# A sixth Strassen pair in each layer's mix, a fused mask and maximum, and a new order of steps, in a two-layer decoder trunk on one core

## The chip, the core and the metric

The kernel runs on one core of one Trainium2 chip. It is timed as a whole: device microseconds from its start to its end, median of three runs. One more execution was taken with the hardware profiler, and everything that is said of engines below comes from that one.

## What is computed

Two layers run on 256 tokens of width 1024, in float32. Each layer does this (norms, gains and masks left out of the sketch):

```python
x += 1/2 * swiglu(rmsnorm(x), w1, w3, w2)            # first feed-forward block, hidden width 2816
h  = rmsnorm(x); P = h @ w_in                         # one projection, cut into rq rk rv rg | sq sk sv | mq | gates
ret = retention(rq, rk, rv) * silu(rg)                # branch A, 4 heads
swa = sliding_window_attention(sq, sk, sv, sinks)     # branch B, 16 query heads of 64, window 128, a sink per head
mo  = memory_attention(mq, mk, mv)                    # branch C, mk and mv from rmsnorm(mem) @ w_mem_kv
x += (g0 * (ret @ w_ur) + g1 * (swa @ w_us) + g2 * (mo @ w_um)) @ w_o
x += 1/2 * swiglu(rmsnorm(x), ...)                    # second feed-forward block
```

In the sliding window attention a score is s = (q.k) / 8 plus a mask of 0 or -1e30. The maximum m of a row is taken over its scores and the head's sink; then come exp(s - m), the row's sum with exp(sink - m) added, and the division.

## The kernel before

**Precision.** A float32 product is made of three TensorE passes. Each operand is split in a rounded part (hi) and the rest (lo), and hi*lo, hi*hi and lo*hi are summed (three_passes, L777 to L779). ScalarE makes w_hi from the raw weights (L1184), VectorE makes w_lo = raw - w_hi (L1586), each in two halves of 1024 columns. A weight unit is 128x2048 numbers, 1 MB.

**Items.** The work is one long list of items. A plain unit (for instance mv0.1: memory values, column half 0, row half 1) is 8 (tile, block) places times 3 passes, 24 matmuls of 512 columns. Two plain chunks of one width can instead be a pair, done by Strassen's method (the Winograd form) in seven products (rk:5, rk:1, and so on), each of 12 matmuls; done as plain units the pair takes 96 matmuls, as products 84. Products 5, 6, 7 and 4 need a sum of weight quarters. Such a sum is made by VectorE in the raw buffer (L1583, a 128x2048 addition), or, where the table ADDED names it, by an accumulating DMA issued from GpSimd (L714). A product also needs its own rounding and its own rest, as a unit does, so that a pair needs 7 of these where plain units need 4. Products 3, 5, 6 and 7 read sums of the activations (S_hi, S_lo), made once in each block.

**The ring.** In the mix the rounded weights lie in three places (w_hi, w_lo), taken in turn. So the place for item o comes free when TensorE has finished item o-3: after item X of the list, ScalarE rounds item X+3 and VectorE then makes its rest. Raw weights lie in three places of their own, and some other buffers are lent to them while they are idle (RAW_B, RAW_Q, RAW_X, RAW_A); their loads go through SyncE's queue in list order.

**The order.** SCHEDULE is one string, written out by hand, and all engines walk through it in the same order. For each entry ScalarE and VectorE first evacuate that item's result from its PSUM bank and then do the split that is due behind it. Entries without a dot or colon are steps: `sqt` transposes the attention queries; `s0` to `s3` are the scores of four heads each; `e0` is the exponentials on ScalarE, `n0` the division on VectorE; `pt0` and `pv0` are the transposes and products with the values; `rotq` and `rotk` are the rotations; `S_sum`, `S_hi`, `S_lo` make the activation sums of the mix; `mkt` transposes the memory keys.

**Banks.** Steps take the PSUM banks 4 to 7 in rotation. A score step takes all four, so two score steps with no other step of this kind between them use the same four banks, and TensorE waits for all four before the first matmul of a score step:

```python
for j in range(4):
    pe.wait_ge(*room(l, f"s{g}_{j}"))
```

The transposes `sqt` wait for all of the query chunks' evacuations (`wait_done("sq0", "sq1")`) before the first of them.

**Before the change** five pairs run in each mix (rk, rg, gs, gr, gm). The queries of the local attention are four plain units (sq0.0, sq0.1, sq1.0, sq1.1).

Of the kernel before, what the change touches and what calls it, by code (L numbers as in the profile page):

```python
# [119 lines left out]
ADDED = {(0, 'gm'): (6, 7, 4), (0, 'gr'): (7, 4), (0, 'gs'): (6, 7), (0, 'rg'): (6, 7, 4), (0, 'rk'): (6, 7, 4), (1, 0): (7, 4), (1, 1): (6, 7, 4), (1, 2): (7,), (1, 3): (6, 7, 4), (2, 0): (7, 4), (2, 1): (6, 7, 4), (2, 2): (7, 4), (2, 3): (7,)}  # L120
# [42 lines left out]
def item_of(o):  # L163
    return ITEMS[o // NI][o % NI]
# [25 lines left out]
RAW_B, RAW_Q, RAW_X, RAW_A = (3, 4), (5, 6), 7, 8  # L190
# [32 lines left out]
def plan_weights():  # L223
# [26 lines left out]
    loads, raw_of, held = [], {}, [(-1, None)] * (RAW_A + 1)  # L250
    added_after, added_at, adds, sum_behind = [[] for _ in range(n)], {}, {m: 0 for m in (5, 6, 7, 4)}, {}
    for o in range(n):
# [3 lines left out]
        else:  # L256
# [22 lines left out]
        for unit, key, until in parts:  # L279
            s = min(raw_slots(o), key=lambda v: held[v][0])  # L280
# [9 lines left out]
DVE_STEPS = 28  # L290
# [88 lines left out]
def build(nc, x_in, mem_in, memt_in, stream, gains_in, gfin_in, rot_in, decay_in, mask_in, ident_in, out):  # L379
# [6 lines left out]
    with ctx:  # L386
# [42 lines left out]
        hM = new("hM", [P, KT, SEQ], at=q_at)  # L429
# [1600 lines left out]
```

## Time and profile before

| what | value |
|---|---|
| median of 3 runs | 1439.35 us (1438.45 to 1440.83) |
| the profiled execution, its time | 1438.82 us |
| its span, first to last instruction | 1436.8 us |
| TensorE busy | 1418.4 us |
| VectorE busy | 1170.3 us |
| ScalarE busy | 973.0 us |
| GpSimd busy | 67.9 us |
| granted TensorE clock | 0.998 |

The 2.0 us between the time and the span lie outside of the first and last instruction. Busy time is a union of instruction times. Matmuls overlap in the pipeline, so the distance from start to start is what a matmul costs.

### The profile page before, as it was taken

What the parts mean: (1) busy time and instruction counts of PE and PEld (TensorE: products, weight loads), DVE (VectorE), ACT (ScalarE), POOL (GpSimd) and SP (SyncE); (2) the same over time, 40 slices, a digit from 0 to 9 for tenths busy, and PEclk for the clock granted to TensorE, in tenths of its full rate; (3) what the DMA queues carried; (4) which work ended last, traced back from release to release, by engine and by line L of the source; (5) the groups of instructions that cost most, each with busy time, mean ns of one, the idle gap of its engine ahead of it and who ended that gap; (6) DMA issues with size and microseconds to landing.
All of it is one profiled execution on the core that took longest, in us unless ns stands there. A gap on an engine that the chain in (4) does not pass through costs nothing.

```text
span 1436.8 us, 17632 instructions
## 1 busy us (share of the span) xinstructions
PE 1418.4 (99%) x6654; PEld 1164.8 (81%) x6654; DVE 1170.3 (81%) x1322; ACT 973.0 (68%) x1426; POOL 67.9 (5%) x93
## 2 busy tenths in 40 slices
PE   8999999999999999999999999999999999999997
PEld 6887888878888888888887888887788888888886
DVE  7999756799868769898799987468997778688895
ACT  6777666879656747676577675668785666577663
POOL 0000000000000000000000000000000000000000
PEclk9999999999999999999999999999999999999999
DMA  9998748688668675998849787486785886859861
GB/s 369 269 285 247 265 146 299 195 258 228 204 199 257 233 299 201 280 279 245 278 138 271 260 211 262 172 269 208 224 240 204 248 245 211 325 164 311 254 206 44
DMA packets 49395, 341.39 MB, mean 238 GB/s; under 512 B 5568, under 2 KB 6208, under 8 KB 8608
## 3 DMA queue, kind: packets, MB, share of 16 engines
q1 hardware_dynamic: 37392, 259.54, 48.2%
q0 software_dynamic: 8912, 63.84, 23.4%
q10 hardware_dynamic: 3008, 16.90, 3.0%
q8 instruction: 53, 0.87, 0.2%
q14 instruction: 30, 0.25, 0.0%
HBM read 332.91 MB, written 7.34 MB: 237 GB/s over the span
## 4 chain that ended last, share of the span: by engine, by line
PE 83%; DVE 9%; DMA 4%; issue 2%; ACT 1%; SPq 0%; ACTq 0%; DVEq 0%; POOLq 0%
PE bank L777 25%; PE bank L779 25%; PE bank L778 25%; DVE w_lo L1586 5%; PE bank L834 3%; DMA raw_b<-in_stream 2%; DMA raw<-in_stream 1%; DVE w_lo_more L1586 1%; PE bank L1111 1%; PE bank L1093 1%; PE bank L985 1%; PE bank L997 1%; ACT w_hi L1184 1%; PE bank L1012 1%; DVE raw L1583 1%
## 5 line engine op out<-in xcount | busy, mean ns | idle before, releaser
L1586 DVE TENSOR_TENSOR w_lo<-raw,w_hi 128x1024 fp32r<-128x1024 f32 x338 | 398.1, 1221 | 122.5 <-ACT w_hi L1184 122.0
L1184 ACT ACTIVATE w_hi<-raw 128x1024 fp32r<-128x1024 f32 x338 | 338.9, 1054 | 145.7 <-PE bank L779 130.2
L777 PE MATMUL bank<-w_hi,hT_lo 128*128 128x512 f32 (+1 forms) x684 | 267.9, 392 | 1.3 <-DVE half L1691 1.0
L779 PE MATMUL bank<-w_lo,hT_hi 128*128 128x512 f32 (+1 forms) x684 | 263.4, 385 | 0.0
L778 PE MATMUL bank<-w_hi,hT_hi 128*128 128x512 f32 (+1 forms) x684 | 263.3, 385 | 0.0
L777 PEld LDWEIGHTS bank<-w_hi,hT_lo 128*128 128x128 f32 x684 | 128.6, 188 | 32.1 <-issue 4.2
L777 PE MATMUL bank<-w_hi,S_lo 128*128 128x512 f32 x372 | 148.6, 400 | 1.2 <-ACT snap L1267 1.2
L779 PEld LDWEIGHTS bank<-w_lo,hT_hi 128*128 128x128 f32 x684 | 128.5, 188 | 26.2
L778 PEld LDWEIGHTS bank<-w_hi,hT_hi 128*128 128x128 f32 x684 | 128.7, 188 | 23.9
L779 PE MATMUL bank<-w_lo,S_hi 128*128 128x512 f32 x372 | 145.1, 390 | 0.0
L778 PE MATMUL bank<-w_hi,S_hi 128*128 128x512 f32 x372 | 144.9, 390 | 0.0
L777 PE MATMUL bank<-w_hi,bT_lo 128*128 128x512 f32 x320 | 125.9, 393 | 0.0
L779 PE MATMUL bank<-w_lo,bT_hi 128*128 128x512 f32 x320 | 124.7, 390 | 0.0
L778 PE MATMUL bank<-w_hi,bT_hi 128*128 128x512 f32 x320 | 124.6, 389 | 0.0
L777 PE MATMUL bank<-w_hi,gT_lo 128*128 128x512 f32 x248 | 97.5, 393 | 1.1 <-DVE gT_lo L1604 1.0
L779 PE MATMUL bank<-w_lo,gT_hi 128*128 128x512 f32 x248 | 96.7, 390 | 0.0
L778 PE MATMUL bank<-w_hi,gT_hi 128*128 128x512 f32 x248 | 96.5, 389 | 0.0
L1586 DVE TENSOR_TENSOR w_lo<-raw_q,w_hi 128x1024 fp32r<-128x1024 f32 x78 | 92.0, 1223 | 5.0 <-ACT w_hi L1184 5.0
L1184 ACT ACTIVATE w_hi<-raw_q 128x1024 fp32r<-128x1024 f32 x78 | 78.3, 1055 | 24.4 <-PE bank L779 16.5
L777 PEld LDWEIGHTS bank<-w_hi,S_lo 128*128 128x128 f32 x372 | 69.9, 188 | 15.8 <-ACT snap L1267 2.1
L779 PEld LDWEIGHTS bank<-w_lo,S_hi 128*128 128x128 f32 x372 | 69.8, 188 | 15.0
L778 PEld LDWEIGHTS bank<-w_hi,S_hi 128*128 128x128 f32 x372 | 70.0, 188 | 13.7
(231 smaller groups left out, 2460.7 us busy)
## 6 DMA issues: line engine op xcount, KB each, us to landing
raw<-in_stream SPq DMA_DIRECT2D x149, 1024.0 KB, 5.8
raw_q<-in_stream SPq DMA_DIRECT2D x34, 1024.0 KB, 7.1
raw_b<-in_stream SPq DMA_DIRECT2D x31, 1024.0 KB, 7.3
raw<-in_stream POOLq DMA_DIRECT2D x29, 1024.0 KB, 8.5
raw_x<-in_stream SPq DMA_DIRECT2D x18, 1024.0 KB, 4.9
raw_b<-in_stream POOLq DMA_DIRECT2D x14, 1024.0 KB, 10.3
raw_a<-in_stream SPq DMA_DIRECT2D x12, 1024.0 KB, 6.8
raw_q<-in_stream POOLq DMA_DIRECT2D x9, 1024.0 KB, 10.9
```

What stands on the lines that cost most here:

```text
L777: nc.tensor.matmul(dst, xl, wh[:, a:b], start=first, stop=False, skip_group_check=more)
L778: nc.tensor.matmul(dst, xh, wh[:, a:b], start=False, stop=False, skip_group_check=more)
L779: return nc.tensor.matmul(dst, xh, wl[:, a:b], start=False, stop=last, skip_group_check=more)
L834: last = nc.tensor.transpose(bank(name)[:, at:at + P], src(t, k0 + j), ident[:, :])
L985: last = nc.tensor.matmul(bank(name)[:, i * n:(i + 1) * n], sqT[rows, head // 2, tokens(b)], skT[rows, head // (SWA_H // SWA_KV), 0:n], st ...
L997: last = nc.tensor.transpose(bank(name)[:, i * P:(i + 1) * P], prob[:, g % 2, head, part * P:(part + 1) * P], ident[:, :])
L1012: nc.tensor.matmul(o, v, heads[:, :, odd, 0:2, :], start=True, stop=False, skip_group_check=True)
L1093: last = nc.tensor.matmul(bank(name)[:, t * MEM:(t + 1) * MEM], mqT[:, 2 * h + k, tokens(t)], mkT[:, 2 * h + k, :], start=k == 0, stop=k == 1)
L1111: last = nc.tensor.matmul(bank(name)[:, j * SEQ:(j + 1) * SEQ], mv[:, m, k * P:(k + 1) * P], mpT[:, h, m, :], start=m == 0, stop=m == 1)
L1184: nc.scalar.activation(slots(o)[0][:, part], raw_slot(s)[:, part], ACT.Copy).then_inc(hi_split, 1)
L1583: nc.vector.tensor_tensor(raw_slot(to[0]), raw_slot(to[0]), raw_slot(plus[0]), ALU.add).then_inc(weights_made, 1)
L1586: nc.vector.tensor_tensor(lo[:, part], raw_slot(s)[:, part], hi[:, part].bitcast(F32), ALU.subtract)\
```

## The change

The pair sq (its chunks sq0 and sq1) becomes a sixth pair. Only one of its sums, that of product 7, goes by DMA; those of 5, 6 and 4 are made by VectorE. Two sums of other pairs also move from DMA to VectorE in each layer (rk:6 in both layers, gm:4 in both layers). The units of mv move ahead, among the products of sq. The four stretches of mask, scale and maximum are fused: one tensor_tensor_reduce for each head and block does the scaling, adds the mask, and gives the row's maximum with the sink as its start value. Both raw_q places are lent to the first part of the mix, and a new place raw_s (over srg, after `re`) to its last part. hM moves from the raw_q region to that of sqT. Two waits are added in the feed-forward blocks before act_s and act_g are written again; both name work of the chunk before.

```diff
-mk0.1+xt0 mk1.0+xt1 skv.0 mk1.1 sq0.0 S_sum S_hi S_lo mkt sq0.1 sq1.0 skt sq1.1 mv0.0 sqt rk:5 s0 mv0.1 rk:3 e0 s1 mv1.0 mv1.1 e1 n0 n1 rk:1 rv0.0 pt0 rk:6 pv0 pt1 rk:7 mv_out rk:2 s2 rk:4 rg:5 pv1 e2 n2 rotq rv0.1 s3 rv1.0 rg:3 rqt rg:1 pt2 e3 rotk rg:6 rg:2 pv2 rv1.1 rg:7 n3 mq1.0 rkt rg:4 gs:5 pt3 gs:3 rs ...
+mk0.1+xt0 mk1.0+xt1 S_sum mk1.1 skv.0 mkt S_hi S_lo mv0.0 sq:5 sq:1 sq:3 sq:6 mv0.1 mv1.0 mv1.1 skt sq:7 sq:2 sq:4 sqt rk:5 s0 rk:3 e0 s1 n0 rk:1 e1 n1 rv0.0 pt0 rk:6 pv0 mv_out pt1 rk:7 rk:2 s2 rk:4 rg:5 pv1 rg:3 rv0.1 e2 s3 n2 rotq rv1.0 rg:1 pt2 e3 rg:6 rqt rotk rg:2 rv1.1 rg:7 pv2 rkt n3 mq1.0 rg:4 gs:5 pt3 gs:1 gs:3 rs ...
-ADDED = {(0, 'gm'): (6, 7, 4), ..., (0, 'rk'): (6, 7, 4), ...}
+ADDED = {(0, 'gm'): (6, 7), ..., (0, 'rk'): (7, 4), (0, 'sq'): (7,), ...}
+Q_ITEMS = {RAW_Q[0]: (AT[0]["mix", 0] + 3, min(AT[0]["mix", UNIT_AT[c, 1]] for c in ("mv0", "mv1")) + 1),
+           RAW_Q[1]: (AT[0]["mix", 0] + 3, RV_ITEM + 1)}
+S_ITEMS = item_after("re") + 2, item_after("mpt")
@@ sync: loads into lent places wait for the work that used them
+                if s == RAW_Q[0] and part_of(item) == 0 and not again and o < NI:
+                    sp.wait_ge(mem_msq_ready, TT)
+                if s == RAW_Q[1] and part_of(item) == 0 and not again:
+                    sp.wait_ge(memt_lo, o // NI + 1)
+                if s == RAW_S and (owner is None or o // NI != owner // NI):
+                    sp.wait_ge(*out_of(o // NI, "ro_3"))
@@ feed-forward, ScalarE and VectorE
+                            if behind is not None:
+                                act.wait_ge(*out_of(l, f"up{f}_{behind}t{t}"))
+                        if behind is not None:
+                            dve.wait_ge(*full(l, f"gt{f}_{behind}"))
@@ VectorE, steps s0 to s3
-                            nc.vector.scalar_tensor_tensor(dst, src, HD ** -0.5, msk, op0=ALU.mult, op1=ALU.add)\
-                                .then_inc(free(name), 1)
+                            for i in range(2):
+                                head, at = 2 * i + odd, G_SINK + GRP * g + 2 * i + odd
+                                last = nc.vector.tensor_tensor_reduce(
+                                    pr[:, head, 0:WIN] if b == 0 else pr[:, head, WIN:3 * WIN], bank(name)[:, i * w:(i + 1) * w],
+                                    mask[:, WIN:] if b == 0 else mask[:, :], HD ** -0.5, gains[:, l, at:at + 1],
+                                    ALU.add, ALU.max, smax[:, par, head, b:b + 1])
+                            last.then_inc(free(name), 1)
-                        nc.vector.tensor_reduce(smax[:, par, :, 0], pr[:, :, 0:WIN], axis=AXX, op=ALU.max)
-                        own(nc.vector.tensor_reduce(smax[:, par, :, 1], pr[:, :, WIN:3 * WIN], axis=AXX, op=ALU.max))
-                        settled()
-                        own(nc.vector.tensor_tensor(smax[:, par], smax[:, par], sink, ALU.max))
-                        settled()
```

## Rows read from the trace of the kernel before

**Rows 1.** Part 1 of the page: busy us, share of span, instructions

```profile
PE 1418.4 (99%) x6654; PEld 1164.8 (81%) x6654; DVE 1170.3 (81%) x1322; ACT 973.0 (68%) x1426; POOL 67.9 (5%) x93
```

**Rows 2.** Busy time by stretch: length, then PE, PEld, DVE, ACT, POOL, clock, DMA

```profile
0.00:190.50 190.50, 183.04 (x818) 147.58 (x819) 159.41 (x176) 127.89 (x171) 11.28 (x22) 1.00 0.86 281
190.50:243.90 53.40, 53.40 (x278) 45.50 (x277) 34.11 (x37) 38.18 (x62) 2.40 (x6) 1.00 0.60 229
243.90:353.40 109.50, 109.44 (x554) 86.99 (x553) 95.92 (x126) 86.00 (x158) 5.66 (x7) 1.00 0.78 228
353.40:543.90 190.50, 190.50 (x893) 159.05 (x892) 144.47 (x170) 118.84 (x173) 7.03 (x8) 1.00 0.74 242
720.70:899.20 178.50, 176.63 (x796) 144.53 (x797) 155.43 (x165) 123.34 (x163) 9.43 (x11) 1.00 0.76 230
952.60:1062.10 109.50, 109.44 (x553) 86.98 (x552) 95.89 (x125) 85.96 (x158) 5.70 (x7) 1.00 0.79 228
```

**Rows 3.** Timeline of TensorE, layer 0: end of mv0.0, sqt, rk:5, s0, mv0.1

```profile
249.09 0.39 PE L779 MATMUL bank<-w_lo,bT_hi 128*128 128x512 f32 x1
249.32 1.91 PE L834 MATMUL bank<-ident,stB 128*128 128x128 f32 x16
250.99 0.48 PE L777 MATMUL bank<-w_hi,S_lo 128*128 128x512 f32 x1
...
253.35 0.39 PE L778 MATMUL bank<-w_hi,S_hi 128*128 128x512 f32 x1
253.58 0.39 PE L779 MATMUL bank<-w_lo,S_hi 128*128 128x512 f32 x1
253.90 1.58 PE L985 MATMUL bank<-skT,sqT 64*128 64x128 f32 x16
255.41 0.50 PE L777 MATMUL bank<-w_hi,bT_lo 128*128 128x512 f32 x1
```

**Rows 4.** Timeline, ScalarE and VectorE behind rk:5, and s1 on TensorE

```profile
254.00 0.69 ACT L1396 ACTIVATE stB<-bank,rstd 128x512 f32<-128x512 f32 x1 [0.47 <-PE bank L779]
254.59 2.00 ACT L1184 ACTIVATE w_hi<-raw 128x1024 fp32r<-128x1024 f32 x2
255.67 2.36 DVE L1586 TENSOR_TENSOR w_lo<-raw,w_hi 128x1024 fp32r<-128x1024 f32 x2 [2.64 <-ACT w_hi L1184]
257.95 1.94 DVE L1849 SCALAR_TENSOR_TENSOR prob<-bank,mask 128x256 f32<-128x256 f32 x4
260.02 0.69 DVE L1853 TENSOR_REDUCE smax<-prob 128x4 f32<-128x512 f32 x1
260.63 1.21 DVE L1854 TENSOR_REDUCE smax<-prob 128x4 f32<-128x1024 f32 x1
261.87 0.17 DVE L1857 TENSOR_TENSOR smax<-smax,gains 128x8 f32<-128x8 f32 x1
262.07 0.17 DVE L1859 TENSOR_SCALAR snm<-smax 128x8 f32<-128x8 f32 x1
262.15 0.16 DVE L1860 TENSOR_TENSOR ssink<-gains,smax 128x8 f32<-128x8 f32 x1
263.47 0.39 PE L779 MATMUL bank<-w_lo,S_hi 128*128 128x512 f32 x1
263.79 1.58 PE L985 MATMUL bank<-skT,sqT 64*128 64x128 f32 x16
```

**Rows 5.** Timeline: TensorE waits for a bank that ScalarE copies out

```profile
47.11 0.39 PE L779 MATMUL bank<-w_lo,S_hi 128*128 128x512 f32 x1
48.19 0.50 PE L777 MATMUL bank<-w_hi_more,S_lo 128*128 128x512 f32 x1 [0.69 <-ACT snap L1267]
47.54 0.60 ACT L1267 ACTIVATE snap<-bank 128x512 f32<-128x512 f32 x1 [0.23 <-PE bank L779]
```

**Rows 6.** Groups by form on VectorE, 243.9 to 351.2: busy us, mean ns

```profile
L1586 DVE TENSOR_TENSOR w_lo<-raw,w_hi 128x1024 fp32r<-128x1024 f32 x27 | 31.8, 1220 | 8.8 <-ACT w_hi L1184 8.8
L1849 DVE SCALAR_TENSOR_TENSOR prob<-bank,mask 128x512 f32<-128x512 f32 x8 | 5.1, 684 | 0.0
L1849 DVE SCALAR_TENSOR_TENSOR prob<-bank,mask 128x256 f32<-128x256 f32 x8 | 3.0, 418 | 0.0
L1583 DVE TENSOR_TENSOR raw<-raw,raw_a 128x2048 f32<-128x2048 f32 x1 | 2.3, 2284 | 0.0
L1797 DVE SCALAR_TENSOR_TENSOR stB<-bank,minus_rstd,stB 128x512 f32<-128x512 f32 x2 | 1.5, 748 | 0.0
```

**Rows 7.** Timeline of VectorE: short operations from PSUM, back to back

```profile
362.12 0.42 DVE L1879 TENSOR_TENSOR sdec<-bank,decay 128x256 f32<-128x256 f32 x1
362.45 0.28 DVE L1880 TENSOR_TENSOR sdec<-bank,decay 128x128 f32<-128x128 f32 x1
362.65 0.42 DVE L1879 TENSOR_TENSOR sdec<-bank,decay 128x256 f32<-128x256 f32 x1
```

**Rows 8.** Timeline of ScalarE: exponentials that also give a row sum

```profile
268.30 0.49 ACT L1488 ACTIVATE prob<-prob,snm 128x256 f32<-128x256 f32 x1
268.69 0.19 ACT L1488 ACTIVATION_READ_ACCUMULATOR prob<-prob,snm 128x1 f32 x1
268.79 0.39 ACT L1488 ACTIVATE prob<-prob,snm 128x128 f32<-128x128 f32 x1
```

**Rows 9.** Part 6 of the page: DMA issues, KB each, median us to landing

```profile
raw_q<-in_stream SPq DMA_DIRECT2D x34, 1024.0 KB, 7.1
raw<-in_stream POOLq DMA_DIRECT2D x29, 1024.0 KB, 8.5
```

**Rows 10.** Groups by form on ScalarE, 243.9 to 353.4: evacuations

```profile
L1337 ACT ACTIVATE stB<-bank,rstd 128x512 f32<-128x512 f32 x1 | 0.7, 689 | 1.9 <-PE bank L779 1.9
L1405 ACT ACTIVATE stB<-bank,rstd 128x512 f32<-128x512 f32 x1 | 0.7, 689 | 2.4 <-PE bank L779 2.4
```

More of the change, by code:

```diff
@@ L216, in raw_slots @@
         slots.append(RAW_A)
+    if PAIRS[0] and part_of(item_of(o)) == 0:
+        slots += [s for s in RAW_Q if Q_ITEMS[s][0] < i < Q_ITEMS[s][1]]
+    if PAIRS[0] and S_ITEMS[0] < i < S_ITEMS[1]:
+        slots.append(RAW_S)
     return slots
@@ L240, in plan_weights @@
     for o in range(n):
-        item = item_of(o)
-        if item[0] == "prod" and item[3] in SUMS and item[3] not in added(item):
+        l, item = o // NI, item_of(o)
+        if item[0] == "prod" and item[3] in SUMS and item[3] not in added(l, item):
             sums_first[o - SUM_EARLY.get(item[3], 1)].append((item[:3], item[3]))
@@ L262, in plan_weights @@
                 for p in SUMS:
-                    if p not in added(item) and SUMS[p] == q:
+                    if p not in added(l, item) and SUMS[p] == q:
                         until = max(until, sum_at[l, item[:3], p])
@@ L270, in plan_weights @@
                 for p in SUMS:
-                    if p not in added(item) and SUMS[p] == WEIGHT[m]:
+                    if p not in added(l, item) and SUMS[p] == WEIGHT[m]:
                         count = max(count, sum_at[l, item[:3], p])
                 sum_behind[l, item[:3], m] = count
-            if m in added(item):
+            if m in added(l, item):
                 adds[m] += 1
@@ L279, in plan_weights @@
         for unit, key, until in parts:
-            s = min(raw_slots(o), key=lambda v: held[v][0])
+            lent = {RAW_A: A_ITEMS, RAW_S: S_ITEMS, **Q_ITEMS, **dict.fromkeys(RAW_B, B_ITEMS)} if part_of(item) == 0 else {}
+            s = min([v for v in raw_slots(o) if v not in lent or until <= lo_at[l * NI + lent[v][1] - 1]], key=lambda v: held[v][0])
             loads.append((o, l * NU + unit, s, held[s], until))
@@ L610, in sums_no, with plain_behind @@
             return (2 + mix) * l + (0, 1 + mix)[f - 1] if f else 3 * l + 1
+        def plain_behind(l, f, c):
+            order = [s[2] for s in ffn_steps(l, f) if s[0] == "up" and s[3] == 1]
+            return order[order.index(c) - 1] if order.index(c) else None
         QUARTERS = {2: (0, 0), 6: (0, 1), 4: (1, 0), 7: (1, 1)}
```

41 lines of the change are left out of this document (26 added, 15 removed).

## The prediction

> **What bounds the kernel now.** I read the shares of busy time first, then busy time by stretch of the schedule, then the timeline at the places that the change touches. [Rows 1] show TensorE busy for 1418.4 of the 1436.8 us. Matmul times overlap, so I take the distance between starts: 253.35 to 253.58 is 0.23 us, and one product of 12 matmuls, rk:5, runs from 250.99 to about 253.80, where its last start (253.58) plus one step ends [rows 3]. Twelve steps of 0.227 us are 2.72 us, and a plain unit of 24 is 5.44 us. That step holds wherever two 512-wide matmuls follow each other with no wait between.
>
> By stretch [rows 2] the mix of layer 0 is full: 53.40 of 53.40, 109.44 of 109.50 and 190.50 of 190.50 us. TensorE is idle for 7.5 us in the first feed-forward block, where the kernel starts up, and for 1.9 us in that of layer 1. So in the mix there is next to no wait that any change could remove. What the change can win there is work taken from TensorE, and every new wait of TensorE in the mix is paid in full, because nothing later has slack to give back.
>
> The second thing to see in [rows 2] is VectorE. It is busy for 34.11 of 53.40 us before 243.9 and for 95.92 of 109.50 us from 243.9 to 353.4, where the local attention lies. Layer 1 repeats this to a tenth (95.89). The clock is 1.00 throughout.
>
> **What is removed from TensorE.** Four units (96 matmuls) become seven products (84). That is 12 x 0.227 = 2.72 us per layer, 5.44 us in all. No transposes and no activation sums are added: S_hi and S_lo are there for the other pairs.
>
> **What is added on VectorE for the pair.** Three more splits of two halves at 1.22 us each (2.36 us with their overlap [rows 4, 6]), three sums at 2.28 us and three evacuations at 0.75 us [rows 6]: 7.1 + 6.8 + 2.2 = 16.1 us per layer. They fall in the stretch where VectorE is idle for 53.40 - 34.11 = 19.3 us [rows 2]. TensorE gets 4 x 5.44 us of mv units there as well, against 4 x 2.36 us of VectorE, so on the whole the pair is hidden. Locally it is less roomy: between `skv.0` and sq:3 VectorE must do S_lo (about 2.5 us), the sum for sq:6 and two splits. By the same walk as below I find the rest for sq:3 about 0.4 us late.
>
> **The transposes of the queries.** Before, a whole unit (mv0.0) stood between the last query unit and sqt, and the timeline shows no gap at 249.32 [rows 3]. Now sqt stands right behind sq:4. TensorE has to wait for ScalarE to see the end of sq:4 (0.2 us, as 253.80 to 254.00 [rows 4]) and to copy 0.69 us [rows 10]. The nearest wait of this form in the trace is that at 47.11 to 48.19, start to start 1.08 us instead of 0.23, so 0.85 us lost, with a 0.60 us copy [rows 5]. With 0.69 us it is 0.95 us per layer, and 0.85 at least.
>
> **The second score step is where the sum is decided.** s0 and s1 take the same four banks, and s1 waits until all four are free. Before, TensorE had mv0.1 and rk:3 between them, 8.2 us. Now it has rk:3 alone. I count from the end of rk:5 (253.80). TensorE does s0 in 1.60 us (253.80 to 255.41 [rows 3]) and rk:3 in 2.72, and asks for s1 at +4.32. VectorE must first make the rest of item rk:5 + 3, and this waits for the ring place that rk:5 frees: ScalarE copies rk:5 out, rounds from +0.79 to +2.79, VectorE makes the rest, and it begins on the scores of s0 at +4.15 (257.95 [rows 4]). That chain is the same after the change, with rv0.0 in place of mv1.0. Queued behind it on VectorE are the masks, so the banks come free only at 4.15 + X, where X is the time of the masking.
>
> X was 1.95 us for four operations (257.95 to 259.89 [rows 4]); the maxima came behind the release of the banks. Now the maximum is inside: eight operations, four of 128 and four of 256 columns, and nothing is released before its second head is done. The trace does not show this operation. From below: plain operations of these two widths out of PSUM start 0.33 and 0.20 us apart [rows 7], so 4 x 0.53 = 2.1 us. From above: no overlap, the 256-wide one 0.42 us and the 128-wide one 0.28 us [rows 7], each with 0.06 us for a pointer operand (748 against 684 ns [rows 6]) and 0.17 us for reading the maximum out as a small operation of its own [rows 4]: 4 x 0.65 + 4 x 0.51 = 4.6 us. Between the two, ScalarE's exponentials are the nearest row, since they also write a per-row result: the read adds about 0.1 us to the step [rows 8]. With 0.1 us for the read and 0.06 for the pointer, X = 2.1 + 8 x 0.16 = 3.4 us. The wait is 4.15 + X + 0.1 for the restart - 4.32: 3.3 us per layer, between 2.0 and 4.5.
>
> The Trainium skill bears on X (VectorE: DVE Perf Modes, section "Two Vector instructions with no wait between them"): an operation that also writes out its accumulator is two instructions. By it a group has 8 + 8 + 2 = 18 VectorE instructions where it had 9, which speaks against the fusion. No row here shows such a pair on VectorE; on ScalarE the reading instruction is there [rows 8]. The same page ("The DRAIN you can't avoid") has the next operation start only when the pipeline is empty; here the next one starts 0.09 us before the end of the one before [rows 7], and the rows decide. By that page X would be 4 x (0.42 + 0.28) = 2.8 us without the reads.
>
> **The rest of the local attention.** A group's VectorE time goes from 4.29 us (257.95 to 262.31, less overlap [rows 4]) to X + 0.25 = 3.65, so 2.6 us less over four groups. Against that the sum for rk:6 comes from the DMA (2.2 us). Four mv units leave the stretch: 21.8 us of TensorE, but only 9.1 us of VectorE. So the stretch of 109.5 us becomes 87.7 us of TensorE and 95.9 - 9.1 + 2.2 - 2.6 = 86.4 us of VectorE. VectorE had 13.6 us of room and has 1.3, while it has unavoidable idle pieces such as the 2.64 us before its split in [rows 4]. The wait at s1 already gives it 3.3 us. I take 1.4 us per layer for all further waits here and at sq:3 (the candidates are pv0, pt2, which needs n2, and rg:2), between 0 and 4.
>
> **Edits at nothing.** The added waits of the feed-forward blocks name work that TensorE and VectorE finished a chunk earlier. If they did bind, each would cost about a copy, 0.6 us, in 4 blocks. The lent places let raw loads start earlier; SyncE's queue may stand at the wait for mem_msq_ready, but the DMA engines are busy for only 0.60 of that stretch [rows 2], so the queue has room to catch up. If that cover were gone, a late load would cost up to its 7.1 us to landing [rows 9], in layer 0 alone. One DMA sum in each layer less on GpSimd's queue (8.5 us each [rows 9]) frees bandwidth that nobody waits for. The sum for gm:4 lies in the stretch with 144.47 of 190.50 us on VectorE [rows 2]: 2.3 us in 46 of room, hidden.
>
> **The sum.** Per layer -2.72 + 0.95 + 3.3 + 1.4 = +2.9 us, twice is +5.9 us. On the profiled execution (1438.8 us, of which 1436.8 are its span) that is 1444.7 us; it was 0.5 us under the median, so 1445.2 us. Bounds: all low, 2 x (-2.72 + 0.85 + 2.0) = +0.3, or 1439.6; all high, 2 x (-2.72 + 1.0 + 4.5 + 4.0) = +13.6, or 1453.
>
> **The rivals.**
> - *The waits at their floor, no change* (chance 0.24). X is near 2.1 us, the shorter groups give VectorE 2 x 1.3 us more room and the 1.4 us vanish. For it: short operations do overlap [rows 7]. Against: the read of the maximum. 1439.6 us.
> - *The banks are free in time, and the kernel is faster* (0.20). Should VectorE reach the masks of s0 before it has to make the rest of rv0.0, it begins right behind s0, at +1.8, and frees the banks at about +4.3 for X = 2.5: the wait at s1 is gone. Then -5.44 + 2 x 0.95 gives 1435.8, with the transposes hidden too 1433.9. It decides at a start before +2.9 us, where the sum of waits per layer falls under the 2.72 us saved by more than 1.4. Against: the ring of three ties that split to rk:5, and VectorE's order is that of the list.
> - *VectorE becomes the bound of the whole stretch* (0.14, part of slower). X is at 4.6 us and over: s1 waits 4.5 us and the stretch another 4: 1453.
> - The forecast itself has 0.42.
>
> **How the numbers follow.** About 0.2% (2.9 us) is what a measurement of this kernel can tell from no change. Slower by more: 0.56 (the forecast and the bound rival); within: 0.24; faster: 0.20. The range leaves out the faster rival and the far end of the bound one: 1437 to 1452. The forecast's own range is 1442 to 1449.
>
> **What would show it.** L777 to L779 have 24 matmuls fewer in all (8 each). In both layers TensorE has a gap of about 3 us before L985 of s1, released by VectorE's masks, and one of about 0.9 us before the 16 transposes of sqt, released by ScalarE. VectorE is busy above 95% from sqt to rg:7. The masks take some 3.4 us for eight, with a small read behind each. I am wrong if s1 starts without a gap, or if a raw load is late behind mem_msq_ready.

## The result, and the profile after

The changed kernel took 1444.07 us, median of 7 runs (1442.04 to 1445.80), the kernel before 1439.35 us beside it (1438.33 to 1441.66, 7 runs). The ratio is 1.0032, with an interval of 1.0023 to 1.0040. It is 4.7 us slower, which is more than the 2.9 us that a measurement can tell from no change. The prediction was +5.9 us. The profiled execution after took 1444.07 us, with a span of 1442.3 us, so the spans differ by 5.5 us.

Part 1 of the page of the changed kernel, to be held against [rows 1]:

```profile
PE 1415.9 (98%) x6630; PEld 1161.0 (80%) x6630; DVE 1200.2 (83%) x1422; ACT 985.1 (68%) x1438; POOL 66.3 (5%) x91
```

TensorE has 24 matmuls fewer, 12 in each layer. Yet its busy time fell by 2.5 us only, not by 5.4, and its idle time (span less busy) rose from 18.4 to 26.4 us, by 8.0. So two things are to be found: 8.0 us of new idle time, and 2.9 us of matmuls that take longer.

The waits of TensorE in the local attention, layer 0 (262 to 310 us) first, then layer 1 (975 to 1030 us). Columns are the total, how often, and the longest:

```profile
PE bank L1008 <- DVE smax L1885: 2.5, 1, 2.5
PE bank L857 <- issue: 0.8, 1, 0.8
PE bank L1035 <- ACT pT L1447: 0.3, 1, 0.3
...
PE bank L1008 <- DVE smax L1885: 2.5, 1, 2.5
PE bank L857 <- issue: 0.8, 1, 0.8
PE bank L1035 <- ACT pT L1447: 0.8, 1, 0.8
```

L1008 are the scores (L985 before), L857 the transposes (L834), L1035 the products with the values (L1012). The kernel before had none of these waits. They sum to 7.7 us over both layers, nearly all of the new idle time. The first is the wait of s1 for its banks, released by the fused masks. The second is sqt right behind sq:4. The third is pv0, which waits for ScalarE's copies of the transposed probabilities (pT).

The wait before sqt on TensorE, with ScalarE's copy of the last product of the queries (timeline, layer 0; start and duration):

```profile
262.57 0.39 PE L802 MATMUL bank<-w_lo,hT_hi 128*128 128x512 f32 x1
263.78 1.94 PE L857 MATMUL bank<-ident,stB 128*128 128x128 f32 x16 [0.82 <-issue]
...
262.99 0.69 ACT L1437 ACTIVATE stB<-bank,rstd 128x512 f32<-128x512 f32 x1 [0.65 <-PE bank L802]
```

From the last start of sq:4 to the first of sqt are 1.21 us instead of 0.23, 0.98 us lost. The profile names "issue" as releaser, but the program has the transposes wait for this copy, and they start 0.1 us after its end (262.99 + 0.69 = 263.68): the copy is the cause. Layer 1 lost the same 0.98 us.

ScalarE and VectorE behind rk:5, and s1 on TensorE, in layer 0. This answers to [rows 4]:

```profile
269.10 2.00 ACT L1207 ACTIVATE w_hi<-raw_b 128x1024 fp32r<-128x1024 f32 x2
...
270.18 2.36 DVE L1620 TENSOR_TENSOR w_lo<-raw_b,w_hi 128x1024 fp32r<-128x1024 f32 x2 [0.96 <-ACT w_hi L1207]
272.46 0.34 DVE L1885 CUSTOM_DVE_ANT_0 prob<-bank,mask,gains 128x128 f32<-128x128 f32 x1
272.73 0.08 DVE L1885 DVE_READ_ACCUMULATOR2_ANT smax<- 128x1 f32 x1
272.73 0.34 DVE L1885 CUSTOM_DVE_ANT_0 prob<-bank,mask,gains 128x128 f32<-128x128 f32 x1
...
273.55 0.48 DVE L1885 CUSTOM_DVE_ANT_0 prob<-bank,mask,gains 128x256 f32<-128x256 f32 x1
...
273.95 0.48 DVE L1885 CUSTOM_DVE_ANT_0 prob<-bank,mask,gains 128x256 f32<-128x256 f32 x1
...
275.17 0.08 DVE L1885 DVE_READ_ACCUMULATOR2_ANT smax<- 128x1 f32 x1
...
272.55 0.39 PE L802 MATMUL bank<-w_lo,S_hi 128*128 128x512 f32 x1
275.39 2.36 PE L1008 MATMUL bank<-skT,sqT 64*128 64x128 f32 x16 [2.46 <-DVE smax L1885]
```

The masks begin at 272.46, which is 4.15 us behind the end of rk:5 (268.31, its last start at 268.09 plus 0.22 as in the prediction); the prediction had 4.15. They start 0.27 us apart at 128 columns and 0.41 us apart at 256, with a read of 0.08 us inside that step, and the last bank is free at 275.25. So X, the time of the masking in the prediction, is 2.8 us.

The last row shows something that was not foreseen: s1 took 2.36 us in layer 0. Before, it was 1.58 [rows 4]. Windows of the changed kernel around s1, layer 0, layer 1, and then the whole stretch from rk:5 to behind rg:7 in layer 0 (columns as in [rows 2]):

```profile
272.00:275.40 3.40, 0.94 (x7) 0.47 (x5) 3.26 (x18) 2.43 (x3) 0.00 (x0) 1.00 0.97 198
275.40:277.60 2.20, 2.20 (x16) 1.58 (x16) 2.20 (x4) 2.17 (x6) 0.00 (x0) 0.65 0.58 119
277.60:281.40 3.80, 3.80 (x15) 3.02 (x14) 3.60 (x22) 2.98 (x14) 0.86 (x1) 0.76 0.45 65
...
988.00:990.00 2.00, 2.00 (x18) 1.59 (x19) 2.00 (x4) 1.97 (x6) 0.00 (x0) 1.00 0.67 139
...
265.50:353.00 87.50, 84.75 (x429) 66.03 (x428) 79.10 (x149) 69.72 (x140) 4.43 (x6) 0.98 0.71 204
```

The granted clock is 1.00 while TensorE stands idle ahead of s1. It is 0.65 in s1 and 0.76 in the 3.8 us behind it, and then 1.00 again, so for some of this time TensorE ran at 1.2 GHz, the lower of its two levels, instead of 2.4. s1 and rk:1 together took 1.7 us longer for it. The same gap in layer 1 (2.46 us) is followed by a clock of 1.00. These 1.7 us are the larger part of the 2.9 us that matmuls took longer; another 0.4 us in layer 0 and 0.8 us in layer 1 I could not place. All of this is read from one execution: the mean granted clock of the seven executions lies between 0.995 and 0.998, so how much of the median's 4.7 us is the clock is not shown.

Added up over both layers: -5.4 for the saved matmuls, +2.0 before sqt, +4.9 before s1, +1.1 before pv0, +1.7 for the clock and +1.2 unplaced. That is +5.5 us, the difference of the spans. Outside the mixes, one wait of 1.0 us in the first feed-forward block of layer 1 is new, for a raw load that landed late. Small differences of the other sign in the other feed-forward blocks and at the ends make up for it.

### The profile page after: what moved, and what is told of

The parts are those of the page before. It is cut to its first block, busy times and chain, and to the rows that moved or that the text cites. A ratio compares the mean times of both kernels' runs of the same rounds, so it can differ in the third digit from the quotient of the medians.

```text
span 1442.3 us, 17758 instructions
## 1 busy us (share of the span) xinstructions
PE 1415.9 (98%) x6630; PEld 1161.0 (80%) x6630; DVE 1200.2 (83%) x1422; ACT 985.1 (68%) x1438; POOL 66.3 (5%) x91
## 4 chain that ended last, share of the span: by engine, by line
PE 83%; DVE 8%; DMA 3%; ACT 3%; issue 2%; SPq 0%; ACTq 0%; DVEq 0%; POOLq 0%
PE bank L800 25%; PE bank L802 25%; PE bank L801 25%; DVE w_lo L1620 4%; PE bank L857 3%; DMA raw_b<-in_stream 2%; ACT w_hi L1207 1%; DMA raw<-in_stream 1%; DVE w_lo_more L1620 1%; PE bank L1134 1%; PE bank L1116 1%; ACT prob L1520 1%; PE bank L1008 1%; PE bank L1035 1%; PE bank L1020 1%
## 5 line engine op out<-in xcount | busy, mean ns | idle before, releaser
L1620 DVE TENSOR_TENSOR w_lo<-raw,w_hi 128x1024 fp32r<-128x1024 f32 x314 | 369.4, 1219 | 88.8 <-ACT w_hi L1207 88.2
L1207 ACT ACTIVATE w_hi<-raw 128x1024 fp32r<-128x1024 f32 x314 | 315.1, 1054 | 129.0 <-PE bank L802 111.1
L800 PE MATMUL bank<-w_hi,hT_lo 128*128 128x512 f32 (+1 forms) x644 | 253.0, 393 | 2.7 <-DVE act_a L1685 1.0
L802 PE MATMUL bank<-w_lo,hT_hi 128*128 128x512 f32 (+1 forms) x644 | 248.0, 385 | 0.0
L801 PE MATMUL bank<-w_hi,hT_hi 128*128 128x512 f32 (+1 forms) x644 | 247.8, 385 | 0.0
L800 PE MATMUL bank<-w_hi,S_lo 128*128 128x512 f32 x404 | 161.0, 398 | 1.2 <-ACT snap L1293 1.2
L802 PE MATMUL bank<-w_lo,S_hi 128*128 128x512 f32 x404 | 157.6, 390 | 0.0
L801 PE MATMUL bank<-w_hi,S_hi 128*128 128x512 f32 x404 | 157.4, 390 | 0.0
L1620 DVE TENSOR_TENSOR w_lo<-raw_q,w_hi 128x1024 fp32r<-128x1024 f32 x90 | 105.9, 1217 | 14.8 <-ACT w_hi L1207 14.7
L1620 DVE TENSOR_TENSOR w_lo<-raw_b,w_hi 128x1024 fp32r<-128x1024 f32 x74 | 87.0, 1217 | 8.7 <-ACT w_hi L1207 8.7
```

What stands on the lines that cost most here:

```text
L800: nc.tensor.matmul(dst, xl, wh[:, a:b], start=first, stop=False, skip_group_check=more)
L801: nc.tensor.matmul(dst, xh, wh[:, a:b], start=False, stop=False, skip_group_check=more)
L802: return nc.tensor.matmul(dst, xh, wl[:, a:b], start=False, stop=last, skip_group_check=more)
L1207: nc.scalar.activation(slots(o)[0][:, part], raw_slot(s)[:, part], ACT.Copy).then_inc(hi_split, 1)
L1620: nc.vector.tensor_tensor(lo[:, part], raw_slot(s)[:, part], hi[:, part].bitcast(F32), ALU.subtract)\
```

## The experiments

All were timed beside the kernel before, which took 1439.05 to 1440.06 us there. **Theory 1** was that of the prediction: moving the mv units ahead of the queries takes away what lay over the short waits of the local attention. The rival was that the pair itself or the fused operation costs the time. The first three put mv units back between the waits.

### The order, with the pair kept

```
  after:  ... mv0.1 mv1.0 mv1.1 skt sq:7 sq:2 sq:4 sqt rk:5 s0 rk:3 e0 s1 ...
  e1:     ... mv0.1 mv1.0 skt sq:7 sq:2 sq:4 sqt rk:5 s0 mv1.1 rk:3 e0 s1 ...
  e2:     ... mv0.1 mv1.0 skt sq:7 sq:2 sq:4 mv1.1 sqt rk:5 s0 rk:3 e0 s1 ...
  e3:     ... mv0.1 skt sq:7 sq:2 sq:4 mv1.0 sqt rk:5 s0 mv1.1 rk:3 e0 s1 ...
```

> The changed kernel with one entry moved: mv1.1 stands between s0 and rk:3 instead of before sq:7. Theory 1 (the wait is one for banks that VectorE frees too late): TensorE asks for s1 at 1.6 + 5.44 + 2.72 = 9.8 us behind rk:5, VectorE has freed the banks at 4.15 + 2.8 = 6.9 us, so the 2.5 us gap is gone in both layers, and with it the slow clock behind it in layer 0; the wait before sqt stays. 1444.1 - 5.1 = 1439 us, 1437.5 if the clock's 1.7 us come back too. Theory 2 (VectorE's amount of work bounds the whole stretch, wherever the mv units stand in it): the gap at s1 only moves to later places, 1443 to 1445 us.

> The changed kernel with mv1.1 moved to stand between sq:4 and sqt. Theory 1: the 1.0 us before the transposes goes in both layers, the gap at s1 stays at about 2.5 us: 1442 us. Theory 2 (the transposes wait for something else than ScalarE's copy of sq:4, or the stretch is bound by VectorE): no change, 1443 to 1445 us.

> The changed kernel with mv1.0 between sq:4 and sqt and mv1.1 between s0 and rk:3. Theory 1: both waits go, -5.1 and -2.0 us, and in layer 0 1.7 us of slow clock: 1435.5 to 1437 us, so faster than the kernel before by 2 to 4 us. What stays of the 5.4 us saved is lost to short waits for VectorE's rests (sq:3, pv0, pt2, rg:2), 0.6 to 1.4 us per layer. Theory 2 (VectorE's total binds): 1441 us and over, since its room in the stretch is unchanged.

Measured: e1 1460.92 us (ratio 1.0156, 1.0142 to 1.0169), e2 1453.11 (1.0093, 1.0077 to 1.0108), e3 1461.83 (1.0159, 1.0145 to 1.0173). In each the wait that it was to cover is gone, and the kernel is 9 to 18 us slower than the changed one, which neither theory foresaw. In e1 TensorE waits 4.2 us ahead of pv0, for ScalarE's copies of pT, and 3.0 us ahead of mv1.0, for ScalarE's evacuation of an earlier mv unit. ScalarE's timeline in e1 at the second of them:

```profile
236.53 2.00 ACT L1207 ACTIVATE w_hi<-raw_q 128x1024 fp32r<-128x1024 f32 x2
244.28 2.00 ACT L1207 ACTIVATE w_hi<-raw_x 128x1024 fp32r<-128x1024 f32 x2 [5.75 <-DMA raw_x<-in_stream]
246.19 1.25 ACT L1363 ACTIVATE mv_made<-bank,rstd_mem 128x512 f32<-128x512 f32 x2
```

The rounding at 244.28 is that of sq:7, whose sum of weight quarters is made by an accumulating DMA. With one mv unit fewer in front it is asked for 5.4 us earlier than in the changed kernel, and it is not there: GpSimd issued it at 234.39, once VectorE had done with the buffer, it landed 9.9 us later, and ScalarE stands 5.75 us. Queued behind that rounding is the evacuation of an mv unit, and TensorE needs its bank. So the mv units ahead of sq:7 are not idle cover; they are the time in which that sum arrives. e2 has this wait too (3.4 us). e3, with two units fewer in front, waits 4.8 us there.

The 4.2 us at pv0 in e1 and e3 are the second part of the loss. A unit between s0 and s1 adds its own evacuation and rounding to ScalarE's queue ahead of the exponentials, and the copies of pT come later. The third part is the clock. In the profiled execution of e1 it fell behind each of these waits, in both layers (0.57 over 4.0 us from 247.0, 0.52 over 7.0 us from 295.0, and 0.57 over 4.0 us from 967.0 and again from 1018.0), some 7 us in all of the time in which TensorE worked, where the changed kernel lost 1.7. This is about as much as either kind of wait.

### The parts by themselves

e4 is the changed kernel with the masks and maxima of before (four masks and two reductions for a group, [rows 4]); e5 is the kernel before with the fused operation alone; e6 is the kernel before, the queries still four plain units, with the mv units moved ahead and the rest of that stretch in the new order:

```
- nc.vector.tensor_tensor_reduce(pr[...], bank(name)[...], mask[...], HD ** -0.5, gains[...], ALU.add, ALU.max, smax[...])
+ nc.vector.scalar_tensor_tensor(dst, src, HD ** -0.5, msk, op0=ALU.mult, op1=ALU.add)     # e4; e5 the other way
...
- sq0.0 ... mkt sq0.1 sq1.0 skt sq1.1 mv0.0 sqt rk:5 s0 mv0.1 rk:3 e0 s1 mv1.0 mv1.1 e1 n0 n1 rk:1 rv0.0 pt0
+ sq0.0 ... mkt sq0.1 mv0.0 mv0.1 sq1.0 mv1.0 mv1.1 skt sq1.1 sqt rk:5 s0 rk:3 e0 s1 n0 rk:1 e1 n1 rv0.0 pt0     # e6
```

> The changed kernel with the masks and maxima of the kernel before (four scalar_tensor_tensor, two tensor_reduce, a maximum with the sink) in place of the fused operation. Theory 1 by itself: the four banks of s0 are free after 1.95 us of masking instead of 2.8, so the gap at s1 shrinks by 0.8 us per layer: 1442.5 us. But each group then takes 4.3 instead of 3.2 us of VectorE, 4.6 us more per layer in a stretch that has about 1 us of room: theory 2 has the waits behind s1 (pv0, pt2, rg:2) grow by 3 to 4 us per layer: 1449 to 1451 us. I hold both to act: 1445 to 1449 us.

> The kernel before with nothing changed but the fused mask and maximum. VectorE saves 1.2 us in each of eight groups, 9.6 us in all. Theory 1 (in the mix of the kernel before TensorE waits for nobody): no change, 1438.5 to 1440 us. The rival, that these groups were already on the path that sets the end: up to 9 us faster, 1430 us.

> The kernel before (five pairs, old masks, the queries as plain units) with the four mv units moved ahead of the last query unit, so that sqt stands right behind sq1.1 and only rk:3 stands between s0 and s1, as in the changed kernel. Nothing is saved on TensorE. Theory 1: the order alone brings the waits, 1.0 us at sqt, 1.7 us at s1 (shorter than with the fused masks, since the banks are freed after 1.95 us) and some 2 us per layer behind them at pt0, pv0 and pt2 as with the old masks in the changed kernel: 1447 to 1450 us. The rival, that the waits come from the added weight sums and splits of the sixth pair: 1439 to 1441 us.

Measured: e4 1446.98 us (1.0054, 1.0041 to 1.0066); e5 1440.13 against 1440.06 (1.0004, 0.9996 to 1.0013); e6 1450.17 (1.0074, 1.0062 to 1.0086). e4 lies inside its forecast, e5 and e6 within 0.2 us of the upper end of their first theories.

The waits of TensorE in e6, layer 0:

```profile
PE bank L985 <- DVE prob L1849: 1.6, 1, 1.6
PE bank L997 <- DVE prob L1870: 1.1, 1, 1.1
PE bank L834 <- ACT stB L1337: 1.0, 1, 1.0
PE bank L1012 <- ACT pT L1415: 0.8, 1, 0.8
```

The order alone costs 10 us, and these four waits in two layers are 9.0 us. (In the profiled execution the span grew by 10.9 us; the rest is about 1.7 us of low clock in the first feed-forward block, 0.58 over 4.0 us from 30.0, which e7 and e9 show too and which lies far ahead of the moved units.) Here no pair was added, so this settles where most of the loss is: in the order. In the kernel before, mv1.0 and mv1.1 stood between s1 and pt0, 10.9 us of TensorE work, and the fused operation has nothing to win because nothing waits (e5).

In the changed kernel the fused operation is worth about 3 us (1446.98 against 1444.07), though it makes the wait of s1 longer. The parts do not simply add: 10.1 for the order, -5.4 for the saved matmuls and -2.9 for the fused operation make +1.8 us, and +4.7 was measured. The low clock in layer 0 (1.7), the unplaced 1.2 us and the late raw load (1.0) are of that size, but no run separates them. Between e6 and e4, both with the old masks and the new order up to pt0, stands the pair (and the new order behind it), and e4 is only about 3 us faster, not 5.4; its new wait of 0.7 us a layer at pt2 is 1.4 us of what is missing. The two longest waits of e4 in layer 0:

```profile
PE bank L1008 <- DVE prob L1886: 1.6, 1, 1.6
PE bank L1020 <- DVE prob L1907: 1.1, 1, 1.1
```

The old masks free the banks 0.85 us earlier, since the maxima come behind the release. But the waits at pt0 and pv0 (1.1 and 0.8) come back, and one of 0.7 at pt2. e4 does have one thing better: its clock stays 1.00 behind a gap of 1.6 us.

### Masks first

VectorE makes the masks of s0 ahead of the split that is due behind rk:5 (e7), and those of s1 ahead of the split behind rk:3 as well (e8). The first is the rival of the prediction in which the banks are free in time:

```
+ held = {"s0": 5}                      # e8: {"s0": 5, "s1": 3}
  if s[0] == "step":
      step(s[1])
+     if s[1] in held:
+         splits(l, AT[l]["prod", 0, "rk", held[s[1]]])
      continue
  if s[0] == "prod":
      product(*s[2:])
-     splits(l, AT[l][s])
+     if s[2] != "rk" or s[3] not in held.values():
+         splits(l, AT[l][s])
```

> The changed kernel, in which VectorE does the masks of s0 before the rest of item rv0.0 (the split due behind rk:5) instead of after it; nothing else moves. The masks then start when s0 is done, at +1.7 us behind rk:5 instead of +4.15, and the banks are free at about +4.5, just after TensorE asks for them. Theory 1: the gap at s1 goes (2.5 us in each layer, and the slow clock behind it in layer 0), 1444.1 - 5 = 1439 us or a little less. Theory 2 (the chain masks, exponentials, division, transposes runs at VectorE's and ScalarE's pace): the masks of s1 still wait behind two splits, so TensorE catches up with pt0 and pv0 earlier and waits there instead: only 1 to 2 us come back, 1442 to 1443 us.

> As e7, and the masks of s1 also before the split due behind rk:3 (that of rk:6). Theory 1 alone has nothing more to gain over e7. By theory 2 the chain of both groups now starts earlier: division n0 done at the time that TensorE reaches pt0, a wait of about 1 us left at pv0: 1438.5 to 1441 us, clearly under e7.

Measured: e7 1450.79 us (1.0075, 1.0062 to 1.0087), e8 1450.26 (1.0075, 1.0063 to 1.0087). My expectation fell: I had both as a gain, e8 clearly ahead of e7, and e7 lost 6.7 us against the changed kernel. Its second theory had the place right, waits before pt0 and pv0, and not their size. The waits of e7 in layer 0, and rows of ScalarE's and GpSimd's timelines, also of e7:

```profile
PE bank L1035 <- ACT pT L1447: 3.8, 1, 3.8
PE bank L1020 <- DVE prob L1904: 1.6, 1, 1.6
PE bank L857 <- issue: 0.8, 1, 0.8
```

```profile
274.78 2.01 ACT L1207 ACTIVATE w_hi<-raw_a 128x1024 fp32r<-128x1024 f32 x2 [0.93 <-DVE raw_a L1617]
276.81 1.28 ACT L1516 ACT_TABLE_LOAD   x1
...
283.43 2.01 ACT L1207 ACTIVATE w_hi<-raw 128x1024 fp32r<-128x1024 f32 x2 [1.03 <-DMA raw<-in_stream]
...
275.30 0.87 POOL L737 DMA_DIRECT2D raw<-in_stream  x1 [40.36 <-DVE raw_a L1617]
```

The wait of s1 is gone, as it was meant to be, and 5.3 us stand in front of pt0 and pv0 instead. VectorE makes the sum of raw_a (L1617) behind the masks of s0 here (from 272.45; from 266.94 in the changed kernel). ScalarE's rounding waits 0.93 us for that sum, and the exponentials stand behind the rounding. The same sum holds back GpSimd's accumulating DMA, which is issued at 275.30 instead of 269.77, and a later rounding waits another 1.03 us for it. Layer 1 has both waits (0.92 and 0.91 us), and they make up nearly all of the 2.06 us by which pv0 comes later there (table below). From that rounding on ScalarE has hardly any idle time in the changed kernel. In layer 1 it has no idle time at all from 985.50 to the last copy of pT at 1002.5 (the rows of the exponentials are not shown):

```profile
985.50 0.69 ACT L1428 ACTIVATE stB<-bank,rstd 128x512 f32<-128x512 f32 x1 [1.87 <-PE bank L802]
986.09 1.99 ACT L1207 ACTIVATE w_hi<-raw_a 128x1024 fp32r<-128x1024 f32 x2
988.10 1.28 ACT L1516 ACT_TABLE_LOAD   x1
...
993.59 1.99 ACT L1207 ACTIVATE w_hi<-raw 128x1024 fp32r<-128x1024 f32 x2
...
999.10 2.00 ACT L1207 ACTIVATE w_hi<-raw_x 128x1024 fp32r<-128x1024 f32 x2
1000.99 1.54 ACT L1447 ACTIVATE pT<-bank 128x512 f32<-128x512 f32 x3
```

It is set off by the end of rk:3 (985.47) and takes 17 us to pT. So whatever delays that chain delays pv0, and TensorE coming early to s1 does not help. 1.28 us of the chain are the ACT_TABLE_LOAD at 988.10; no run shortened the chain, so what a shorter one would give is not shown. In layer 0 the chain has one idle piece of 1.0 us, because it had to wait for rk:1, which the low clock had slowed. The time of e8 differs from that of e7 by nothing that can be measured. In e7, behind the wait at pv0, the clock is 0.61 over 4 us in layer 0; in layer 1 it is 0.50 over 4 us and 0.76 over the next 4. That is about 1.6 and 2.8 us of the time in which TensorE worked, most of the rest of the loss in that execution.

### Is it ScalarE's chain?

That gave a new theory, and the last four runs are for it: what bounds the stretch from s0 to pv0 is ScalarE's chain, wherever TensorE waits for it.

```
  after:  ... mv0.1 mv1.0 mv1.1 skt sq:7 sq:2 sq:4 sqt rk:5 s0 rk:3 e0 s1 n0 rk:1 e1 n1 rv0.0 pt0 ... rg:3 rv0.1 e2
  e9:     ... mv1.1 sq:7 sq:2 sq:4 skt sqt ...
  e10:    ... sqt rk:5 s0 rk:3 rv0.0 e0 s1 n0 rk:1 e1 n1 pt0 ...
  e11:    ... mv1.1 sq:7 sq:2 sq:4 skt sqt rk:5 s0 rk:3 rv0.0 e0 s1 n0 rk:1 e1 n1 rv0.1 pt0 ... rg:3 e2
  e12, grp_scores:
-     for j in range(4):
-         pe.wait_ge(*room(l, f"s{g}_{j}"))
      for b in range(2):
+         for j in (2 * b, 2 * b + 1):
+             pe.wait_ge(*room(l, f"s{g}_{j}"))
```

> The changed kernel with one step moved: the transposes of the local keys (skt) stand behind the last product of the query pair instead of ahead of its sq:7 product, so that they run while ScalarE's copy of that product's bank is made. Theory 1 (the 1.0 us that each layer loses ahead of sqt is the wait for that copy and nothing else): the wait shrinks by the skt transposes' own 0.4 us, in both layers, and nothing behind it moves; 1443.0 to 1444.0 us, ratio to before 1.0025 to 1.0035. Rival (the slack so won is lost again at the next wait, that before s1, which is set by VectorE's chain and not by when the TensorE comes to it): the wait before s1 grows by as much; 1444.0 to 1444.7.

> The changed kernel with one unit moved: rv0.0 (16 matmul triples, 5.44 us) stands between rk:3 and the scores s1 instead of between e1 and pt0. Nothing is added, and what lies between s0 and pv0 is the same work. Theory 1 (the run before this one showed that with the wait of s1 gone the wait comes back before pt0 and pv0: what bounds the stretch from s0 to pv0 is ScalarE's chain of exponentials, splits and copies of the transposed probabilities, wherever the TensorE waits for it): no gap before s1, 2 to 5 us before pt0 and pv0 instead, 1443 to 1447 us, ratio 1.003 to 1.006. Theory 2 (each wait is its own, and one covered is won): 1438.5 to 1440.5, as before the change or faster.

> The changed kernel with rv0.0 ahead of s1, rv0.1 (another 5.44 us) taken from behind pv1 and put ahead of pt0, and skt between sq:4 and sqt: between s0 and pv0 there is now 5.4 us more for the TensorE while ScalarE's chain runs. Theory 1 (ScalarE's chain bounds that stretch, by 2.8 to 3.3 us a layer in the changed kernel): the gaps before s1, pt0 and pv0 sum to under 1 us a layer, the granted clock doesn't fall, and as long as nothing opens behind pv1, 1437 to 1440 us, ratio 0.998 to 1.0005. Rival (rv0.1 was the cover of the second group of heads behind pv1, and the evacuation and splits it brings lengthen ScalarE's chain by as much): new waits of 1 to 3 us before pv0, pv1 or pt2, 1441 to 1446.

> The changed kernel, in which the scores wait for the first two of their banks only, and for the other two ahead of the second half of their matmuls (before, for all four at the start). The short masks free the first two first, so the first half of s1 starts about 1.5 us earlier, and the idle time before s1 comes in two pieces of about 1 us. Theory 1 (ScalarE's chain sets when pv0 can start; the drop of the granted clock in layer 0 behind the 2.45 us gap is a second cost by itself): the layers' waits sum to the same, the clock behind s1 stays at 0.95 or more in both layers, 1442.3 to 1444.0. Theory 2 (the s1 wait is a cost by itself): 0.5 to 0.7 us a layer less beside the clock, 1440.8 to 1442.3. Rival (the clock falls for the lack of work whatever the pieces): still 0.65 to 0.8 behind s1 in layer 0, 1443.5 to 1444.5.

Measured: e9 1444.70 us (1.0035, 1.0022 to 1.0048), e10 1451.52 (1.0082, 1.0069 to 1.0094), e11 1451.47 (1.0080, 1.0065 to 1.0094), e12 1443.65 (1.0024, 1.0015 to 1.0033), each against 1439.92.

**e12** is the cleanest test. s1 comes 1.6 us earlier in both layers, counted from the end of sq:4. If that wait were a price by itself, pv0 would come earlier too. The time from the end of sq:4 to the first matmul of pv0, from the timelines:

| | layer 0 | layer 1 |
|---|---|---|
| changed kernel | 28.40 us (clock down behind s1) | 27.30 us |
| e12 | 27.94 us (clock down behind s1) | 27.29 us |
| e7 | 29.49 us | 29.36 us |
| e4 | 27.77 us | 27.76 us |

In layer 1, where the clock plays no part, the start of pv0 did not move by more than 0.01 us: the idle time of s1 shrank from 2.46 to 1.74 us (0.84 and 0.90), TensorE was through with s1 0.43 us earlier, and the wait of pv0 grew from 0.80 to 1.25. So the theory holds for e12. Its time lies inside the span of the changed kernel's runs; a gain is not shown. The clock fell here too, though no single gap was over 1.0 us, where theory 1 had it stay at 0.95 or more; this part came as the rival had it. In layer 1 the same two gaps left it at 1.00. Windows of e12, layer 0:

```profile
276.30:278.00 1.70, 1.70 (x9) 1.06 (x10) 1.70 (x4) 1.67 (x4) 0.00 (x0) 0.68 0.79 164
278.00:280.00 2.00, 2.00 (x6) 1.52 (x6) 2.00 (x10) 2.00 (x11) 0.74 (x1) 0.50 0.01 0
```

**e9.** The wait before sqt shrank, as expected, from 0.82 to 0.39 us, but a new one came in the middle of sqt (timeline of e9):

```profile
263.38 0.60 PE L857 MATMUL bank<-ident,skd 128*128 128x128 f32 x4
264.36 1.50 PE L857 MATMUL bank<-ident,stB 128*128 128x128 f32 x12 [0.39 <-issue]
266.69 0.55 PE L857 MATMUL bank<-ident,stB 128*128 128x128 f32 x3 [0.83 <-ACT skT L1447]
```

skt takes one bank and sqt four, of the same four in rotation, so the last four transposes need the bank of skt. ScalarE copies skT only behind a rounding of 2.0 us. With skt's own 0.6 us taken off, pv0 starts 0.4 us later than in the changed kernel in both layers. Neither theory had this, and the time cannot be told from that of the changed kernel.

**e10** has no wait before s1 and one of 5.0 us before pt0, where the new theory put it (2 to 5), but the time is 4.5 us over what I gave. (The unit has 24 matmuls, eight threes and not sixteen; its 5.44 us are right.) ScalarE's queue has the rounding below ahead of the exponentials of s0, and it waits 2.92 us for a place in the ring, which comes free when TensorE has finished the unit that I had moved (timeline of e10):

```profile
278.82 2.01 ACT L1207 ACTIVATE w_hi<-raw 128x1024 fp32r<-128x1024 f32 x2 [2.92 <-PE bank L802]
```

The clock added to it: 0.51 over 7.0 us behind the wait of layer 0 and 0.51 over 6.2 us behind that of layer 1, some 3 us each.

**e11** has 5.4 us more of TensorE work ahead of pv0 and its time lies above both expectations: the waits before s1 and pt0 are gone, and pv0 waits 4.4 us. The rival named this mechanism, but had 1 to 3 us. Two units and skt were moved at once, so the run prices none of these moves by itself; e9 shows that skt brings 0.83 us in the middle of sqt, and e11 has that wait too. There the copies of pT stand behind the evacuation of the very unit that was to be the cover (timeline of e11, ScalarE):

```profile
292.10 1.23 ACT L1363 ACTIVATE rv<-bank,rstd 128x512 f32<-128x512 f32 x2
293.23 1.99 ACT L1207 ACTIVATE w_hi<-raw_x 128x1024 fp32r<-128x1024 f32 x2
295.13 1.53 ACT L1447 ACTIVATE pT<-bank 128x512 f32<-128x512 f32 x3
```

So the theory needs a correction. ScalarE's chain is not a fixed amount of work that runs beside TensorE. It is a queue in order, and every unit put in front of pt0 puts its evacuation and a rounding, and through the ring a wait for TensorE itself, in front of the exponentials and of the copies of pT. Cover for TensorE and delay for ScalarE come in one piece. In the kernel before, mv1.0 and mv1.1 stood between s1 and e1, behind the exponentials of s0, and there the cover held. This is a reading of the timelines: an order that keeps e0 ahead of the moved unit, or the copies of pT ahead of the rounding, was not tried. No kernel run here beats the kernel before.

## Why the prediction was right, and where it was not

**The saved product** (-2.72 us a layer): 24 matmuls fewer, right. **The pair's work on VectorE** shows no wait of TensorE in the changed kernel, as predicted, though it may stand behind some of the unplaced time; the wait at sq:3 that I feared did not come, the first half of its rest was ready 0.2 us ahead of TensorE.

**sqt** (+0.95 us a layer): measured 0.98 in both layers, by the mechanism given.

**s1** (+3.3 us a layer): the place, the releaser and the start of the masks (4.15, measured 4.15) are right, and X is the mis-sized term. I had 3.4 us; it was 2.8, and the wait 2.45 us instead of 3.3. The error is in the read: I put 0.1 us for it and 0.06 us for the pointer on each of eight operations. The step of 0.27 us at 128 columns is 0.07 more than the plain operation's 0.20, and 0.41 at 256 is 0.08 more than 0.33 [rows 7]. Read and pointer together are 0.08, half of what I took.

The Trainium skill (VectorE: DVE Perf Modes, section "Two Vector instructions with no wait between them") has an operation that also writes out its accumulator as two instructions. The trace agrees, the DVE_READ_ACCUMULATOR2_ANT of 0.08 us is there behind each. By the section "The DRAIN you can't avoid" X was to be 2.8 us if each operation waits for an empty pipeline, which is what was measured, but not for that reason: here an operation of 0.34 us starts 0.27 us after the one before it, so they overlap, and the sum agrees by chance. The prediction left out how that passage of the section ends, that a next operation which is not held starts earlier; with this the trace agrees.

**The further waits** (+1.4 us a layer, between 0 and 4): pv0 was on my list and is the one that came (0.3 and 0.8 us); pt2 and rg:2 did not. With the unplaced 0.4 and 0.8 us the term is 0.7 and 1.6 us. My reason for it was wrong, though. I argued from VectorE's share, which I put above 95% from sqt to rg:7. It was 79.1 of 87.5 us, 90%, hardly another share than that of the same steps before (88.9 of 98.0 us from 251 to 349). What bounds pv0 is ScalarE, of which I had written nothing but copies. That the chain also stands behind the wait of s1, so that the two are one loss at two places, is shown by e12 in layer 1; e7, e10 and e11 fit, but each of them also lengthened the chain.

**What was missing** is the clock. 1.7 us in layer 0 came from a fall of the granted clock behind the new gap. It took back what the shorter wait of s1 had given: -0.85 x 2 on the one side, +1.7 on the other. The further waits came to 2.3 us where I had 2.8, for a reason that I had wrong. That the total came within 1.2 us of the forecast is in part luck.

**The rivals.** "The banks are free in time" needed VectorE to reach the masks first. e7 did that, and it was slower: freeing the banks is not enough when ScalarE's exponentials stand behind the sum that VectorE puts off. "VectorE becomes the bound" did not come. "The waits at their floor" had X at 2.1, and it was 2.8. The added waits of the feed-forward blocks bound nowhere; a raw load was late once in layer 1 (1.0 us), by an amount that went from 0 in e4 to 1.3 us in e12, so it is no firm part of the change.

## What to carry to other kernels

A unit in an order written by hand is cover at one place and a deadline at another: before moving it, write down which wait it hides where it stands, what it pushes back in each engine's own queue, and what needs its time to arrive (here a DMA sum, which three mv units in front gave time to). When a wait of TensorE is covered, follow the engine that released it to the next thing that TensorE needs from it; if that engine runs without idle time from here to there, the wait will only move. Run the new order alone, on the old work, before the arithmetic that it was made for: here the order alone cost 10 us and the saved products were worth 5.4.

## What the hardware showed that was not expected

- The granted clock fell behind short gaps of TensorE, and not always behind gaps of one length. Behind 2.46 us it was 0.65 over 2.2 us and 0.76 over the next 3.8 in layer 0 and stayed 1.00 in layer 1; behind 1.6 us (e4, e6) it stayed in both layers; behind two gaps of 0.84 and 0.90 us with 0.7 us of work between (e12) it fell to 0.68 and 0.50 in layer 0 and stayed in layer 1; behind 3.0 us (e1) it was 0.57 over the next 4 us, and behind 3.6 us in layer 1 of e8 it stayed, as these rows of the windows of e1 and e8 show. Where it fell behind a wait of 3 to 5 us, that cost some 1.5 to 3 us on top of the wait (0.57 over 4.0 us is 1.7 us, 0.51 over the 6.2 us behind the wait of layer 1 in e10 is 3.0). What decides between the two layers I can't say.

```profile
247.00:251.00 4.00, 4.00 (x11) 3.14 (x12) 4.00 (x4) 2.33 (x3) 0.00 (x0) 0.57 0.57 193
...
1008.70:1012.70 4.00, 4.00 (x26) 2.90 (x27) 4.00 (x4) 3.70 (x6) 0.00 (x0) 1.00 0.96 346
```

- The fused mask and maximum on VectorE (CUSTOM_DVE_ANT_0) takes 0.34 us at 128 columns and 0.48 at 256 out of PSUM, and starts every 0.27 and 0.41 us with its read inside. A group of heads takes 3.16 us of VectorE (272.46 to 275.62), where the masks, reductions and small operations of before took 4.36, although it has twice the instructions.
